# A hybrid decoder step on one core: four V steps ahead of the last projection tile, V steps doubled at every fourth duo, 26 selected blocks issued by SyncE instead of GpSimd

## The reference, cut to what matters

```
o_c, o_s = nsa_cmp_sel(q_n, pos, kc, vc, cend, kv_sel[:, :, 0], kv_sel[:, :, 1], overlap)
o_w = window_attend(q_n, win_all[:, :, 0], win_all[:, :, 1], pos, kpos_w)
k_all = jnp.concatenate([gather(cache_dk), k_d], axis=1)
v_all = jnp.concatenate([gather(cache_dv), v_d], axis=1)
o_d = diff_attend(q_d, k_all, v_all, pos, jnp.arange(past + T), lam)
y = layer_output(x, o_n, g_n, z_n, o_d, z_d, lam_init, lp)
```

## Time and profile before

| | |
|---|---|
| median of 3 runs | 760.35 us (760.13 to 760.53) |
| time of the profiled execution | 762.04 us |
| its span, first to last instruction | 760.3 us |
| TensorE busy | 703.2 us, 92% |
| VectorE busy | 488.5 us, 64% |
| ScalarE busy | 205.8 us, 27% |
| GpSimd busy | 104.7 us, 14% |
| mean granted TensorE clock | 0.971 |

### The profile page before, as it was taken

How to read it: one execution, slowest core, us unless ns; L and a number is a source line. 1 busy time by engine, 2 the same in 40 slices (tenths; PEclk the granted TensorE clock), 3 DMA queues, 4 the chain that set the end, 5 groups by cost and what they waited for, 6 DMA issues and landing times.

```text
span 760.3 us, 14082 instructions
## 1 busy us (share of the span) xinstructions
PE 703.2 (92%) x4419; PEld 332.8 (44%) x4419; DVE 488.5 (64%) x976; ACT 205.8 (27%) x530; POOL 104.7 (14%) x198
## 2 busy tenths in 40 slices
PE   6969999999999979999999998978898888999996
PEld 2445544454453635443535633425344352343542
DVE  5357673965776548998597449576867657555273
ACT  3031012102012004222321226434545424333100
POOL 0000000000001001010003656603647000000000
PEclk9989999999999999999999999999999978999999
DMA  8997877998999979999959279979999859984721
GB/s 311 378 319 223 315 228 253 327 366 283 318 371 363 397 277 388 400 309 345 344 186 324 68 227 334 304 235 289 288 324 311 282 180 380 358 297 149 299 87 57
DMA packets 131683, 218.46 MB, mean 287 GB/s; under 512 B 17617, under 2 KB 55738, under 8 KB 130394
## 3 DMA queue, kind: packets, MB, share of 16 engines
q1 hardware_dynamic: 103752, 185.76, 71.0%
q10 hardware_dynamic: 20402, 17.02, 7.2%
q0 software_dynamic: 7456, 14.80, 6.0%
HBM read 211.64 MB, written 10.04 MB: 292 GB/s over the span
## 4 chain that ended last, share of the span: by engine, by line
PE 59%; DVE 13%; issue 11%; DMA 6%; ACTq 4%; SPq 2%; POOLq 2%; ACT 1%; POOL 1%; DVEq 0%
PE banks L686 16%; PE banks L644 10%; PE banks L699 5%; PE banks L1068 4%; PE banks L785 4%; PE banks L1189 3%; ACTq L453 3%; DVE att L1944 3%; DMA ring<-in_dk_cache 2%; PE banks L964 2%; PE banks L1006 2%; PE banks L982 2%; PE banks L634 1%; DVE banks L1943 1%; DMA xn<-in_win_v 1%
## 5 line engine op out<-in xcount | busy, mean ns | idle before, releaser
L686 PE MATMUL banks<-ring,xt 128*128 128x512 f32 (+1 forms) x320 | 130.1, 559 | 0.0
L1442 ACT ACTIVATE wide<-banks,att 128x384 f32<-128x384 f32 (+3 forms) x128 | 66.3, 523 | 124.6 <-DVE att L1944 124.3
L686 PEld LDWEIGHTS banks<-ring,xt 128*128 128x128 f32 x320 | 59.2, 190 | 66.6 <-issue 63.1
L476 POOL DMA_DIRECT2D ring<-in_sel_cache x143 | 75.0, 525 | 45.9 <-issue 39.9
L785 PE MATMUL banks<-ring,small 128*32 128x512 f32 x512 | 71.4, 639 | 1.8 <-DMA ring<-in_dv_cache 1.0
L699 PE MATMUL banks<-ring,small 128*32 128x512 f32 x512 | 62.0, 599 | 2.8 <-DMA ring<-in_dk_cache 2.8
L1943 DVE TENSOR_TENSOR banks<-banks,consts 128x256 f32<-128x256 f32 x64 | 27.3, 427 | 54.1 <-PE banks L964 53.6
L686 PE MATMUL banks<-xt,ring 128*128 128x512 f32 x128 | 56.7, 595 | 0.0
L964 PE MATMUL banks<-proj 64*128 64x384 f32 (+7 forms) x256 | 53.0, 492 | 2.9 <-ACT wide L1442 2.9
L1944 DVE TENSOR_REDUCE att<-banks 128x2 f32<-128x768 f32 (+3 forms) x64 | 52.8, 824 | 2.2
L1251 ACT ACTIVATE proj<-banks 128x512 f32<-128x512 f32 (+1 forms) x26 | 14.6, 566 | 145.3 <-PE banks L686 112.5
(11 more groups left out here) (379 smaller groups left out, 929.9 us busy)
## 6 DMA issues: line engine op xcount, KB each, us to landing
ring<-in_dk_cache SPq DMA_DIRECT2D x256, 256.0 KB, 4.8
ring<-in_dv_cache SPq DMA_DIRECT2D x256, 256.0 KB, 4.9
proj<-in_cmp_cache SPq DMA_DIRECT2D x120, 128.0 KB, 5.4
proj<-in_cmp_cache ACTq DMA_DIRECT2D x104, 128.0 KB, 5.8
ring<-in_w_in SPq DMA_DIRECT2D x6, 2048.0 KB, 13.5
ring<-in_sel_cache POOLq DMA_DIRECT2D x143, 32.0 KB, 5.4
ring<-in_w_out SPq DMA_DIRECT2D x2, 2048.0 KB, 11.0
out_s_win<-in_win_nat SPq DMA_DIRECT2D x1, 4088.0 KB
```

What stands on the lines that cost most here:

```text
L476: eng.dma_start(sel_kv[64 * (n % 2):64 * (n % 2) + 64, q % 8, n // 2, :], src["sel_cache"][bass.ds(at, 1), :, :].rearrange("o k n -> (o k) ...
L686: last = mm(banks[:, 3 + n % 2, 0:width(c)], of, by, start=k == 0, stop=k == KC - 1)
L1442: last = A(e_slot(j, c)[:, 0:n], banks[:, 2 * (j % 2) + c, 0:n], ACT.Exp, bias=row_max[:, j % 4, c:c + 1], accum_out=row_sum[:, j % 4, c:c ...
```

## The change

```diff
-        V_EARLY = 2
+        V_EARLY = 4
...
-        V_NONE, V_MORE = (2, 7, 32, 37, 40, 44), (13, 16, 54, 61)
+        V_NONE, V_MORE = (0, 2, 32, 32, 36, 37, 40, 44), (13, 18, 54, 61)
...
-        V_ROUNDS = [j for j in range(DUOS) for _ in range(int(j not in V_NONE) + int(j in V_MORE))]
+        V_ROUNDS = [j for j in range(DUOS) for _ in range((2, 1, 1, 0)[j % 4] - V_NONE.count(j) + V_MORE.count(j))]
...
-        SEL_DMAS, SEL_EARLY, SEL_SHARED = 4 * 2 + 8 * N_TOP, 2 * N_TOP, 3 * N_TOP
-        SEL_MORE, W_OUT_AT = 26, V_EARLY + 3 + next(v for v in range(64) if v >= V_EARLY and V_ROUNDS[v - V_EARLY] > SEL_AT[1] + 4)
+        SEL_DMAS, SEL_EARLY, SEL_SHARED = 4 * 2 + 8 * N_TOP, 4 * N_TOP, 3 * N_TOP
+        SEL_MORE, W_OUT_AT = 28, V_EARLY + 3 + next(v for v in range(64) if v >= V_EARLY and V_ROUNDS[v - V_EARLY] > SEL_AT[1] + 4)
...
             for v in range(64):
+                if v == 4:
+                    for q in (1, 2):
+                        for first, last in ((SEL_FIRST, 6), (6, 10), (10, SEL_LAST)):
+                            sel_ranked(sp, mybir.EngineType.SP, q, first, last)
                 if v == SEL_MORE:
...
-            for q in range(1, 4):
-                sel_load(q)
+            sel_load(3)
```

## The result

| | before | changed |
|---|---|---|
| median of 20 runs each | 759.99 us (753.81 to 767.43) | 766.23 us (760.15 to 774.54) |
| ratio, 95% interval | | 1.0097 (1.0074 to 1.012) |
| profiled execution, its span | 762.04, 760.3 us | 764.35, 762.7 us |
| mean granted clock | 0.971 | 0.966 |

The changed kernel is 1% slower, where 752.4 us, 1% faster, was forecast. The 20 runs of before stand beside those of the changed kernel; their median is 0.4 us under the 760.35 of the table ahead of the change. Ratios here are of fast runs, which leaves out runs over 1.5% above the fastest of the same kernel (2 of the 20 of the changed one). The two profiled executions are only 2.4 us apart in span, less than the medians' 6.2.

What follows compares the result with a forecast made beforehand. TensorE, busy 92% of the span, was taken as the bound, so only idle time and low clock could move. Terms -2.6 - 3.9 - 0.5 - 2.3 + 0.3 + 1.0 = -8.0 us gave 752.4 us, range 749.0 to 759.2.

Steps and rivals of the forecast that it cites:

- What bounds the kernel: Whole kernel: TensorE works 92% of the span, so the change can move only its idle time and low-clock stretches.
- the ledger: Running count, duo by duo, of time gained or lost, with each V step in hand worth 0.99 us.
- Duos 0 to 9, -2.6: VectorE keeps its pace, duo 10 comes 0.3 us later with three more V steps through: 2.6 us gained.
- the low clock moves to a worse place: Rival: gaps of duos 13 to 17 bring a long low clock, +5 us, 757.4 us; chance 0.13.
- Duos 10 to 13, -3.9: Selected blocks land earlier, the selected scores' wait and low clock go, V step 16 waits 0.8: 3.9 us gained.
- the blocks land when they did: Rival at the selected blocks: p_dv's store holds GpSimd, blocks land only 0.3 us earlier; 758.3 us, chance 0.13.
- Duos 14 to 43, -0.5: Doubled V steps cover bank-5 waits, partly offset by late VectorE starts and gaps: 0.5 us gained, bounds -3.0 and +2.0.
- Duos 44 to 47, -2.3: A V step at duo 44 fills 1.0 us of a gap and low clock mostly goes: 2.3 us gained.
- Duos 48 to 63, +0.3: TensorE full; output weights ahead of V steps 49 and 51 cost 0.3 us, bounds -0.5 and +2.0.
- the output weights stand on the path: Rival at V steps 49 and 51: the weights' loads hold up V pages, +11 us, 763.3 us; chance 0.06.
- The clock elsewhere, +1.0: New gaps near duos 6 and 16 bring low clock, costing 1.0 us, bounds 0 and +3.8.

Runs made afterwards that it cites:

- e4: e1 with the stores of p_dv and s_dv moved behind GpSimd's first set of blocks; ratio to before 0.9992.
- e7: The kernel before with 26 blocks moved to SyncE and the stores of p_dv and s_dv late; ratio to before 0.9983.
- g10: e1 with one V step a duo and the stores of p_dv and s_dv late; ratio to before 0.9986.
- m1: e4 with one V step moved from duo 4 to duo 3; ratio to before 0.9993.
- m2: m1 with two V steps ahead of tile 31 instead of four, the other two at duos 32 and 36; ratio to before 0.9909.
- e3: The kernel before with the output weights moved ahead of V steps 49 and 51; ratio to before 1.0063.
- e1: The changed kernel with the output weights ahead of V steps 46 and 48; ratio to before 0.9967, and 1.0029 when run again.
- g9: The changed kernel with the output weights ahead of V steps 48 and 50; ratio to before 1.009.
- n2: m2 with the stores of p_dv and s_dv back right behind tile 31; ratio to before 0.9964.

## Why the prediction was wrong, step by step

*What bounds the kernel.* Right that only idle time and clock could move. But the *full* part fell by about 1 us where the sum had 4 to 6 (by whether the low clock of 473.9 is counted as clock), and *lost* rose by 8 where it was to fall. Below, the ledger is kept on for the two profiled executions, with 0.99 us for a V step in hand. It comes to +1.3 - 4.6 + 1.0 - 2.8 + 9.3, and -1.8 in the tail, +2.4 us in all.

*Duos 0 to 9, -2.6.* This step failed. V steps ahead of tile 31, `p_dv` at once behind it, the low clock of 473.9 gone: all as said, and VectorE started 1.25 us later than before. The term assumed that VectorE then keeps its pace. It didn't: VectorE stood idle five times before duo 10. The first was behind ScalarE's held issues, which made 1.6 us of the gap at duo 3 (2.79 against 1.22), the others in or just behind the 9.8 us at half clock that followed. The ledger gave GpSimd's early `p_dv` a price on GpSimd's queue and none beside ScalarE's issues. Duo 10 came 4.3 us later instead of 0.3, so the term came to 4.3 - 3 x 0.99 = +1.3. How much of it is the store's is not settled, since e4, with the store late, has a low clock there too. The term also took low clock as gone that in fact moved to duos 3 to 7; "the low clock moves to a worse place" was a rival and came true 40 us earlier than it said. Nor did running ahead pay (e7 against g10, m1 against m2).

*Duos 10 to 13, -3.9.* Right in the mechanism: last block issued near 487.4 and landed before VectorE's L2025 asked at 495.93, no wait at the selected scores, clock 1.00. V step 16 waited 0.37 us instead of 0.8. Duo 14 began at 502.48 with three V steps in hand, against 502.80, so the term came to -4.6. The size holds for these two executions only: e3 is the kernel before up to V step 46, and in its execution the same scores waited 1.14 us and took 3.63 instead of 5.32. So 3 of the 4.1 us that the term won back here were that one execution's. The rival "the blocks land when they did" is out: the pause of 4.36 us was a backlog, since it is 3.7 to 6.4 us long in the four other kernels that have pairs 1 and 2 on GpSimd, and with the short queue the store waits for tile 31 alone.

The Trainium skill, "DMA: Bandwidth & Descriptors", section "Issuing engines are not separate DMA queues", says that spreading DMAs over engines saves only the sequencer's time to start them, usually small beside the DMA. Here that time was 22.5 us on GpSimd for 26 issues and the wait of 2.41 us went with it, so for these 32 KB blocks the measurement decides that it was not small.

*Duos 14 to 43, -0.5.* At duo 14 the ledger stood at +1.3 - 4.6 = -3.3 us. At duo 44, where both have the same V steps through, it stood at -2.3: the scores of duo 44 began at 621.27, before at 623.60. So this term came to +1.0, within its bounds. Of the waits in these duos, bank 5's fell by 1.6 us and bank 4's by 1.4; against that stand the pages' 1.29 and 1.77 us at duos 25 and 26 and 1.0 us more for an exponential. The pages were not in the sum, though the trace of before already had its DMA share of 1.08 there.

*Duos 44 to 47, -2.3.* Right: the gap fell from 1.53 to 0.54 us as said and the low clock behind it went. Duo 48's scores began at 633.01 instead of 638.12, again with the same V steps through, so the term came to -2.8. But a low clock of 3.5 us follows at 633 to 637, behind a wait of 2.26 us for VectorE. Duo 44 was to be 7 us earlier and was 2.3.

*Duos 48 to 63, +0.3.* This step failed too, and it decided the sign: the ledger went from -5.1 us at duo 48 to +4.2 behind duo 63, where the output projection's long run began at 720.69 instead of 716.52, so the term came to +9.3. (The tail gave 1.8 back, nearly all by a low clock that, of the two profiles, only that of before has there.) I counted 13 us from issue to use. The first half had 12.3, and V step 49 waited 1.03 us. The second half was issued at 638.74 and V step 51 was due at 648.76, 10.0 us later; its pages were there after 14.6. The duos between are 49, 50 and 51, and in the new table 51 has no V step: the table that doubles at every fourth duo shortens exactly this stretch. The price was 4.6 us of waiting and, behind it, 3.6 of clock in the profile (7.4 us of TensorE's work at 0.52), about 7 us in the runs. This is the rival "the output weights stand on the path" (763.3, chance 0.06), by its mechanism, at about 7 of its 11 us; that 766.2 lies near its 763.3 is partly luck, since the other terms' 8 us did not come either. Its threshold of 14 us, from one row of before, was about right where the page load follows the half at once (e1: 15.2 us and no wait; before: 13.3 and 0.97), but not sharp: e3 had 14.0 and waited 1.40, g9 had 15.1 and waited 2.96. Counted from the pages' own load, they were there after 13.1 us (before), 13.5 (changed), 11.5 (e3) and 14.1 (g9). A term of +0.3 beside a margin already missed by 1 us was not right.

*The clock elsewhere, +1.0.* Against it, and against the 1.7 and 1.3 us of low clock that two other terms expected to win, stand 8 us more lost over the whole kernel in the runs. No bound of this term held that. Part of the error lies in the method: the terms took stretches of low clock out of one execution of before, which lost 22.0 us (760.3 us at 0.971) where its runs lose 16.8 to 18.3 in the mean. Stretches that one execution shows are not all there to be won.

## What to carry to other kernels

Where a large load is slipped into a stream of small ones, recount the time from its issue to the use of what is queued *behind* it each time the order of the stream changes, and take the shortest stretch, not the mean. Work run ahead of its time was worth nothing here, where the DMA share was near 1, and a queue that is freed early starts its next transfer into someone else's peak. Compare kernels by time at full clock and time lost to the clock apart: a change can gain in one and pay it back in the other. And price a stretch of low clock from several executions, not from the one that was profiled.

## What was not expected of the hardware

In the changed kernel, from 2.9 to 5.9 us behind the issue of GpSimd's 1 MB store, its queue had 79.8% of the DMA engines' time (97.2% in n2, from 2.1 to 5.1 us) and the hardware queue's share was 22.7%; meanwhile two DMA issues of ScalarE took 2.57 us instead of 0.49 each, with its compute waiting behind them. It happened in all eight profiles in which the store left right behind tile 31 after a short GpSimd queue (2.2 to 2.8 us), and in none in which it left late or behind a backlog. The share alone does not make the hold: in the kernel before, as long behind its store (457.8 to 460.8 us), GpSimd's queue had 80.2% and the hardware queue 14.5%, and the two issues of ScalarE there took 0.48 and 0.49 us. What the held ones have in common is that they are the first two blocks that ScalarE issues; whether that or something else holds them stays open.

The spread of one kernel's times is nearly all clock: over 18 runs of the changed kernel *full* has a standard deviation of 1.5 us while *lost* runs from 20.5 to 32.3 us, and profiles of the same kernel show low stretches at different places. The Trainium skill, "TensorE: Matmul & The Clock Gate", Part 1, calls the slow start of a kernel variable from run to run and puts its penalty below 1% of a typical span. The losses here are another thing: they lie all along the kernel, 17 to 26 us of 760, 2 to 3.4%. Why the clock falls in one execution and not in the next stays open.
